# The last layer norm's 1/std and beta through TensorE, and an earlier mark for the expert loop's jump back

## The reference

```
hm = x * (1 + sc2) + sh2
f = grouped_moe(hm, router_w, router_b, exp_w_gate[l], exp_w_up[l], exp_w_down[l])
x = layer_norm(DEEPNORM_ALPHA * x + g2 * f, ln2_g[l], ln2_b[l])
```

## Time and profile before

| | us |
|---|---|
| median of 3 runs | 1911.64 (1909.54 to 1913.4) |
| the profiled execution | 1910.68 |
| its span | 1908.9 |
| TensorE busy | 1742.2 (91%) |
| VectorE busy | 508.8 (27%) |
| ScalarE busy | 163.6 (9%) |
| mean DMA rate | 330 GB/s |

### The profile page before, as it was taken

One profiled execution on the slowest core, in us unless ns is written; L12 is line 12 of the kernel. 1 busy time (PEld: TensorE's weight loads), 2 busy tenths in 40 slices (PEclk: granted clock), 3 DMA queues, 4 the chain that ended last, 5 costly groups with the idle time before them and its releaser, 6 DMA issues.

```text
span 1908.9 us, 21645 instructions
## 1 busy us (share of the span) xinstructions
PE 1742.2 (91%) x8982; PEld 954.8 (50%) x8983; DVE 508.8 (27%) x944; ACT 163.6 (9%) x342; POOL 2.5 (0%) x9
## 2 busy tenths in 40 slices
PE   5889999999999999979999979999889888899984
PEld 3337888688888884454433234332243222433321
DVE  0441536655363201151031120211111111112114
ACT  0001013100000000032000002000020000200000
POOL 0000000000000000000000000000000000000000
PEclk9889999999999999989999999999999999999998
DMA  9996984677677634332689996999999999799995
GB/s 384 426 383 171 369 329 206 265 299 327 268 318 301 269 135 198 157 152 85 277 353 428 428 427 291 387 428 428 428 387 428 428 428 428 292 411 406 428 428 216
DMA packets 51002, 629.78 MB, mean 330 GB/s; under 512 B 5776, under 2 KB 8241, under 8 KB 11849
## 3 DMA queue, kind: packets, MB, share of 16 engines
q1 hardware_dynamic: 49768, 623.15, 78.8%
q10 hardware_dynamic: 1120, 5.00, 0.7%
HBM read 624.46 MB, written 3.67 MB: 329 GB/s over the span
## 4 chain that ended last, share of the span: by engine, by line
PE 76%; DMA 16%; DVE 3%; issue 2%; SPq 1%; ACT 1%; ACTq 0%; DVEq 0%
PE bank L942 42%; PE bank L689 20%; PE bank L701 9%; DMA ring<-in_w_down 8%; DMA ring<-in_w_up_gate 7%; PE bank L713 3%; DMA ring<-in_w_in 1%; DVE ada_rows L1565 1%; PE bank L708 1%; SPq L471 1%; PE bank L974 1%; PE bank L755 0%; ACT region_f L1257 0%; SPq L464 0%; DVE region_a L1524 0%
## 5 line engine op out<-in xcount | busy, mean ns | idle before, releaser
L689 PE MATMUL bank<-ring,region_b 128*64 128x512 f32 x1792 | 402.4, 596 | 30.6 <-DMA ring<-in_w_up_gate 22.1
L942 PE MATMUL bank<-region_a,ring 128*128 128x256 f32 x1792 | 390.3, 379 | 0.0
L942 PEld LDWEIGHTS bank<-region_a,ring 128*128 128x128 f32 x1792 | 339.7, 190 | 49.2 <-issue 3.8
L689 PEld LDWEIGHTS bank<-ring,region_b 128*64 128x64 f32 x1792 | 123.9, 137 | 282.5 <-issue 245.4
L701 PE MATMUL bank<-ring,region_f 128*64 128x512 f32 (+1 forms) x1408 | 231.1, 518 | 26.0 <-DMA ring<-in_w_down 18.9
L1565 DVE SCALAR_TENSOR_TENSOR ada_rows<-ring,condT,ada_rows 128x512 f32<-128x512 f32 x293 | 220.2, 751 | 9.9
L701 PEld LDWEIGHTS bank<-ring,region_f 128*64 128x64 f32 (+1 forms) x1408 | 77.9, 127 | 163.0 <-issue 123.8
L1886 DVE TENSOR_TENSOR region_a<-bank,region_a 128x512 f32<-128x512 f32 x128 | 79.5, 683 | 218.8 <-PE bank L713 218.7
L942 PE MATMUL bank<-ring,region_b 128*128 128x512 f32 x256 | 110.3, 592 | 1.3 <-issue 1.3
L942 PE MATMUL bank<-ring,region_a 128*128 128x512 f32 x160 | 76.8, 633 | 8.7 <-DMA ring<-in_w_in 7.1
L942 PE MATMUL bank<-region_e,region_x 128*128 128x256 f32 x256 | 64.0, 416 | 18.8 <-issue 15.9
(11 more groups left out here) (180 smaller groups left out, 849.1 us busy)
## 6 DMA issues: line engine op xcount, KB each, us to landing
ring<-in_w_up_gate SPq DMA_DIRECT2D x112, 2048.0 KB, 21.5
ring<-in_w_down SPq DMA_DIRECT2D x56, 2048.0 KB, 22.3
ring<-in_ada_w SPq DMA_DIRECT2D x44, 2048.0 KB, 11.8
ring<-in_w_in SPq DMA_DIRECT2D x31, 2048.0 KB, 16.3
region_g<-in_w_up_gate SPq DMA_DIRECT2D x16, 2048.0 KB, 22.4
ring<-in_w_branch SPq DMA_DIRECT2D x8, 2048.0 KB, 17.8
ring<-in_w_out SPq DMA_DIRECT2D x8, 2048.0 KB, 11.4
region_g<-in_w_down SPq DMA_DIRECT2D x8, 2048.0 KB, 22.9
```

The source lines that it names most:

```text
L689: last = nc.tensor.matmul(bank_of(x, j)[n * c:n * c + n, 0:2 * m], tokens(x, 8 * half + k), w[:, k % 4, :, m * c:m * c + m], start=(half = ...
L942: return nc.tensor.matmul(out, lhsT, rhs, start=start, stop=stop)
```

## The change

There are two edits. First, the mark for TensorE's jump back stands ahead of the second expert of a turn instead of the fourth. Second, the last norm is made by three engines. VectorE does the statistics and the centring pass (x - mean) * gamma in place, for one half of the tokens after the other, and then puts 1/std onto the diagonal of a 128x128 matrix (the identity times the column 1/std). TensorE first fills all eight PSUM banks with beta (a product of a row of ones with a row of beta, one partition deep), then adds to each the product of the diagonal matrix with a centred piece, which scales each token's row by its 1/std. ScalarE copies each bank to acc and signals out_ready. SP's part is unchanged.

```diff
+NORM_BANKS = (0, 1, 4, 5, *SUM_BANKS)
...
+        scale_of = [work[:, 0:P], work[:, P:2 * P]]
...
                 for le in range(GRP):
-                    if le == GRP - 1:
+                    if le == 1:
                         back_announced = pe.mark_branch_hint_location()
...
             nc.switch_bb("pe_experts_end")
+            pe.wait_ge(s_ln2, 32)
+            for b in range(len(SUM_BANKS)):
+                pe.wait_ge(m_taken[b], (NE // GRP - 1) * BANK_JOBS + GATHER_JOBS + 2 * GRP + 1)
+            for n in range(4 * TT):
+                mm(psum[NORM_BANKS[n]][:, :], ones[0:1, :], ln2b[0:1, n % 4 * 512:(n % 4 + 1) * 512], True, False)
+            for n in range(4 * TT):
+                a, q = n // 4, n % 4
+                if q == 0:
+                    pe.wait_ge(scale_ready, a + 1)
+                pe.wait_ge(centred_ready, n + 1)
+                mm(psum[NORM_BANKS[n]][:, :], scale_of[a], acc[:, a, q * 512:(q + 1) * 512], False, True)\
+                  .then_inc(normed_full, 1)
...
             for a in range(TT):
                 root(TT, a)
+            for n in range(4 * TT):
+                a, q = n // 4, n % 4
+                act.wait_ge(normed_full, n + 1)
+                act.activation(acc[:, a, q * 512:(q + 1) * 512], psum[NORM_BANKS[n]][:, :], ACT.Copy)\
+                   .then_inc(out_ready, 1)
...
-            for a in range(TT):
-                scaled(acc, ln2g, ln2b, a, TT, out_ready)
+                dve.wait_ge(l_var, TT + a + 1)
+                for q in range(4):
+                    part = acc[:, a, q * 512:(q + 1) * 512]
+                    dve.scalar_tensor_tensor(out=part, in0=part, scalar=lmv[:, a, 0:1],
+                                             in1=ln2g[:, q * 512:(q + 1) * 512], op0=ALU.subtract, op1=ALU.mult)\
+                       .then_inc(centred_ready, 1)
+                dve.wait_ge(l_std, TT + a + 1)
+                link(dve.reciprocal(lrstd[:, a:a + 1], lrstd[:, a:a + 1]))
+                dve.tensor_scalar(scale_of[a], ident, lrstd[:, a:a + 1], None, ALU.mult).then_inc(scale_ready, 1)
```

More of the change, by code:

```diff
@@ L406, in program @@
         out_ready = sem("out_ready")
+        centred_ready = sem("centred_part_ready")
+        scale_ready = sem("diagonal_scale_ready")
+        normed_full = sem("normed_part_full")
         block = ctx.enter_context(nc.Block())
```

## The result

| | before | after |
|---|---|---|
| median, both on one chip | 1911.64 us | 1922.33 us |
| ratio, 95% interval | | 1.0056 [1.0042, 1.0069] |
| profiled execution | 1910.68 us | 1925.44 us |
| its span | 1908.9 us | 1923.7 us |

The forecast was 1910.4 with a range up to 1915.5. Both failed: the time lies 12 us above the forecast and 7 us outside the range. The lines L629, L642, L651, L1223, L1239, L1245 and L942 of before are L634, L647, L656, L1228, L1244, L1250 and L947 of after.

What follows compares the result with a forecast made beforehand. Arriving weights (DMA) were taken to set the pace, with TensorE's jump-back stalls costing time between turns. 0 for the jump and -1.2 for the tail took 1911.64 to 1910.4 us; range 1891.5 to 1915.5.

Steps and rivals of the forecast that it cites:

- Rival (2): Return jumps from the extra sections (L642) lose their announcement as code shifts: +4.65 to +6.1 us each of three; chance 0.10.
- beta term of the tail: Last norm on TensorE: eight beta products take 6.9 us, ending at 1895.1, hidden beside VectorE's work.
- sum with the clock halved: Tail's end with TensorE's products at half clock: last copy ends at 1908.15, a loss of 2.4 us.
- that cover: Beta and first-half products on TensorE hidden under VectorE's work, ending at 1898.6, 1.6 us before the second diagonal.
- full clock: TensorE in the tail, at work from 1888.2 to about 1898.7, was taken to run products at 0.86 us each.
- Rival (3): Tail doesn't gain: TensorE's clock low, far jump uncovered; 1914.0 us at worst; shares chance 0.47 with the forecast.
- rest of the tail: Last norm: VectorE's two halves 11.54 us, products at 0.86, copies about 0.60; the tail gains 1.2 us.
- jump edit at 0: TensorE's jump back (L1245): moving its mark gains nothing, as branch L629 still lies between; ends -14.8 and +6 us.
- rival (1): Jump back's announcement works from its new place, saving 14.8 us over three jumps; run about 1892.9 us; chance 0.41.

Runs made afterwards that it cites:

- e3: Kernel before with 17 tiny TensorE products (68 instructions) added behind the loop, old norm kept: 1918.85 us, ratio 1.0036.
- e8: Kernel before, loop still at slot 104, with 34 tiny products (136 instructions) behind the loop: 1913.41 us, ratio 1.0003.
- e2: Kernel after with the jump back's mark at its old place, so the new norm alone: 1924.28 us, ratio 1.0057.
- e4: Kernel after with beta brought in by the identity times beta spread over 128 partitions instead of one: 1918.08 us, ratio 1.0029.
- e5: Kernel before with the loop's first instruction at slot 60 instead of 104, plus 17 tiny products behind the loop: 1895.02 us, ratio 0.9914.
- e7: e4 with the loop's first instruction at slot 60 instead of 104: 1895.18 us, ratio 0.992 against the kernel before.
- e6: Kernel before with only the loop's first instruction moved from slot 104 to slot 60: 1893.71 us, ratio 0.9908.
- e13: Kernel before with only the loop's first instruction moved from slot 104 to slot 30: 1894.32 us, ratio 0.9921.
- e1: Kernel before with only the jump back's mark moved, ahead of the second expert instead of the fourth: 1911.61 us, ratio 0.9999.

## Why the prediction was wrong

- **Rival (2) was what happened, at a chance of 0.10.** It named the place (L642), the cause (code behind the loop shifts the extra sections against the blocks) and a price of 4.65 to 6.1; the stall grew by 3.74. That the target isn't there in time, which it gives as the reason, no run shows. The step that failed is "Against: nothing in the rows shows a stall there now": the section's place in its block before (202) and after (14) could have been counted, and by e3 (14: 4.08 us) and e8 (82: 0.33 us), which only add code behind the loop, the stall goes with its place. It was one stall and not three. The price was also too low in effect: e3 puts the whole at 7 us, 3.7 of the jump, some 2 of the clock, which falls in the pause (to 0.77 in e3 and 0.82 in after over 978 to 992; in after the next 16 products take 5.73 us instead of 3.65), and the rest not followed.
- **The beta term of the tail was mis-sized.** The prediction had 8 x 0.86 = 6.9 us at the full clock; it is 13.6, 1.7 each. The sum with the clock halved (a loss of 2.4) kept beta under VectorE's work; "were that cover gone, each further us would be one of the end" is what happened. The halved clock of that sum is the 0.50 of the earlier trace rows. The full clock was taken because TensorE has work; e2 and after show the clock at half (0.50) while the engine is busy with one-partition products (7.10 of 7.10 us in e2). Rival (3) had the sign and not the size, 2.4: the tail lost 5.8 us in the trace, and the shallow products cost 6.2 between the medians of e2 and e4 (4.3 between those of after and e4, from two sets of runs).
- **The rest of the tail was right.** VectorE's 11.54 was 11.80, the copies 0.60, a bank every 0.86 at the full clock (after's last copies are 0.60 with 0.26 idle between), and with e4's beta the tail gains 0.9.
- **The jump edit at 0 was right by luck**, for a wrong reason: it is not the branch L629 between mark and jump that makes the announcement fail (e5 and e7, 0.36 to 0.38 us with it in between), and moving the loop to slot 60 or 30 made the jump short (0.25 to 0.38 us in e5, e6, e7 and e13), where moving the mark alone did not (e1: 4.92, 6.26, 6.19). That code ahead had been fetched too far by the time of the old mark, which rival (1) thought conceivable, no run shows. By e5 the 14.8 us of rival (1) were there to be had (17.4 and 18.7 between the medians of before and of e5 and e6), from another line of the kernel.
- **The chances.** 0.41 went to rival (1), argued from the places of the other marks; the place of each jump in its block, which could be counted, was not weighed.

Sum, from the runs on one chip (before 1911.60, e3 1918.85, e4 1918.08, e2 1924.28): 7.2 for the placement (e3 less before), 6.2 for the beta products (e2 less e4) and -0.8 for the norm itself (e4 less e3) make 12.7. They add up to e2 less before by construction, so this shares the loss out and doesn't prove it. Between the medians of before and after it was 10.7; by the ratios of e3, e4 and e2 the shares are 0.36%, 0.28% and -0.07%, 0.57% in all.

## What to carry to other kernels

Code put anywhere behind a loop moves every section after it: count where each taken jump on the critical engine stands in its block of 256 before and after, and try the loop at other slots if one lands around an edge; here one number brought 0.9%. Measure each slot: by its place the jump back at 242 looked safe and stalled, and jumps at 9 looked bad and were short. Check a far jump's row for each of its executions, since one of three stalled. And before giving a busy engine cheap products as filler, look at what they do to its clock: eight products one partition deep took 13.6 and 10.6 us (after and e2) where full ones took 8.8.

The best versions are the kernel before at slot 60 (1893.71) and at slot 30 (1894.32); the new norm with full-depth beta at slot 60 (1895.18) can't be told from them. Within this measurement the new norm brings nothing.

## What the runs showed of the hardware

- TensorE's granted clock was 0.50 with the engine busy 7.10 of 7.10 us on products one partition deep, and was 0.99 again from 1907.5, when products 128 deep had taken over (e2, from 1904.46).
- An announced jump took 4.1 us and ended 2.4 us after the start of a 16 KB transfer of code that, by count, is never run (the return in e3 and after). The jumps back took up to 6.6 us (e4), and which block the transfer beside them carries is open. With the weights streaming, the transfer started 1.7 us into after's return jump and 2.4 to 4.1 us into the stalled jumps back; in before it started 0.7 to 1 us behind the unannounced first jump of the experts (L651) at 867.15.
- Shortening the three jumps back by 17 us in all (18.05 - 1.12, before against e5) moved the median by 17.4 us. The clock's rise from 0.97 to 1.00 is in that too; what is clear is that the DMA limit on either side took little of it back.
